# The second layer's expert gate multiplied into the expert rows, and a final stage of gathers and two adds per tile

## The chip, the cores and the metric

The kernel runs on one core of one Trainium2 chip. The metric is the device time of one execution in microseconds. Engines: PE (TensorE, matrix products and transposes), DVE (VectorE), ACT (ScalarE), POOL (GpSimd, which here issues the indirect gathers) and SP (SyncE, which issues plain loads and stores; ACT issues some stores too).

## The reference, cut to what matters

A two-layer backbone over 512 latent and 256 context tokens of width 1024, in float32. Each layer is a mixer (four head groups, an output projection, a gated residual) followed by a mixture of experts. Only latent tokens are needed behind the second layer's mixer. What the change touches is the last residual:

```python
g_top_p, g_top = lax.top_k(g_prob, 1)
e_w = jax.nn.softmax(e_top_l, axis=-1) * g_top_p      # two experts per token
...
out = jnp.zeros((n_tok + 1, d), h.dtype).at[slot_tok].add(y * slot_w[:, None])
...
h_lat = h_lat + mod_l[5] * y_lat.reshape(bsz, n_lat, d_model)
```

`mod_l[5]` is a vector of 1024 gates, one per column, the same for all latent tokens. So a token's result is its residual plus gate times (w0 y0 + w1 y1), where y0 and y1 are the rows that its two experts give.

## The kernel before, in words

The residual `hT` is kept transposed in SBUF: 128 of the 1024 columns lie on the partitions in each of DC = 8 blocks, the tokens along the free axis. A tile is 128 tokens; layer 0 has 6 of them, layer 1 puts out 4. `PS` is PSUM with 8 banks of 512 floats. Each engine runs its own program, written out in Python; semaphores, `S(name)`, order them. What is told here is layer 1.

**Routing (L1219 to L1243, L1693 to L1707, L2290 to L2370).** PE transposes the normalized tokens tile by tile (L1234), ACT copies each to `ftok` and stores it as rows in DRAM (`f_rows`; L1699, L1703). Meanwhile DVE works out which row of which expert each token goes to; PE's slot matmuls (L1241) turn that into the list `slots` (L2362). ACT's exponentials (L1706, L1707) go into the routing weights `wtok` (L2365 to L2370). SP holds the third expert's weight load until `wtok` is ready (L814 to L820).

**Experts (L1253 to L1324, L1709 to L1748, L2372 to L2398).** 15 items, one to each expert position before the last, of two or three sub-blocks of 32 rows each, 40 sub-blocks in layer 1. For each item POOL gathers its token rows from `f_rows` (L2492) and PE transposes them (L1265). Per sub-block g: PE multiplies with the gate and up weights (64 matmuls, L1284); ACT takes the silu (L1722) and DVE multiplies (L2383); PE transposes that (L1294) and DVE copies it (L2389); PE multiplies with the down weights (32 matmuls, L1307) into bank 5 + g % 2; ACT copies the result into `ysb` (L1729, in `y_store`) and, after an item's last sub-block, stores it to `y_rows` in DRAM (L1736). The stages are staggered: in PE's loop step g stand gate/up of g, the transpose of g - 1 and the down product of g - 2. SP loads 6 MB of weights for each expert, through three buffers for gate/up and two for down, each load held until the products of the buffer's last user are through.

**Overflow (L1333 to L1359, L1754 to L1766, L2404 to L2414, L2498 to L2506).** A loop that runs at least once takes one block of 128 rows for tokens that found no place: gather, transposes, 32 matmuls of 512 columns (L1344), silu, multiply, transposes (L1349), 16 matmuls (L1355), two copies of 512 columns from banks 5 and 6 into `ysb`, one on ACT (L1761), one on DVE (L2413), and a store (L1764).

**Combine (L1361 to L1375, L2416 to L2439, L2511 to L2518).** For each tile, POOL gathers the two rows y0 and y1 of each token out of `y_rows` into a pair of buffers `r12`, two pairs in all, so from tile 2 on it waits for `hup`. DVE scales one (L2428) and adds the other scaled (L2429); PE transposes the sum (8 transposes, L1371); DVE adds each 128x128 block, times its gate column `mod4[:, L, 40 + c, 0]`, onto `hT` (8 operations, L2435).

**Output (L1396 to L1404, L1779 to L1783, L2454 to L2458, L834 to L839).** After all tiles of `combine`, PE transposes `hT` back (8 transposes per tile, L1402), ACT and DVE each copy one half (L1783, L2458) into `restok`, which has two buffers, and SP stores the tile (L837) and waits for the landing.

At the kernel's start SP loads two tables, `consts` and `cols`, each on a semaphore of its own.

## Time and profile before

| | us |
|---|---|
| median of 3 runs | 2084.05 (2080.42 to 2088.05) |
| the profiled execution, its own time | 2082.55 |
| its span, first to last instruction | 2080.7 |
| busy in the span: PE, DVE, ACT | 1833.0 (88%), 794.7 (38%), 583.0 (28%) |
| moved by DMA | 361.38 MB, mean 174 GB/s |

How to read the views used below. Times in a view are microseconds from the span's start unless marked ns. The *chain* is the work that ended last, followed back: start, length, what; "issue" is time for which the profile shows no cause. The *waits* list engine, its line and tile, what it waited for: total, times, longest. A *timeline* row has start, length (of the merged run of instructions), engine, line, operation, output tile <- input tiles, shapes, count, and in brackets the idle time before it with what ended it. A row of a *line group by form* has line, engine, operation, tiles, shapes, count, then busy us, mean ns of one, and the idle time before. A *window* row has the stretch and its length, then busy us (and instructions) of PE, PE's weight loads, DVE, ACT and POOL, then the granted PE clock (1.00 is 2.4 GHz, 0.50 is 1.2 GHz), the busy share of the DMA engines and the GB/s that they moved. "SPq" and "ACTq" are the sequencers that issue DMAs.

### The profile page before, as it was taken

Reading aid. Unit: us, or ns where it says so; the run is one execution under the profiler, and the core shown is the slowest. Engines: PE = TensorE matmul, PEld = TensorE weight load, DVE = VectorE, ACT = ScalarE, POOL = GpSimd, SP = SyncE. Lnnn points to the kernel's source line nnn. Section 1 sums busy time; section 2 is a strip of 40 time slices with the busy share of each in tenths; the row PEclk is TensorE's granted clock in tenths of the full one; section 3 lists DMA queues with packets and bytes.
Section 4 is the critical chain, followed back from the end, with each engine's and each line's share of the span. In section 5 each row is a group of like instructions: output and inputs, shape, how many; then the busy total and the mean of one; then the engine's idle time right before and its main releaser. Section 6 shows DMA issues by size and latency. Waiting matters only on the chain.

```text
span 2080.7 us, 36365 instructions
## 1 busy us (share of the span) xinstructions
PE 1833.0 (88%) x15671; PEld 1153.4 (55%) x15671; DVE 794.7 (38%) x1692; ACT 583.0 (28%) x1232; POOL 84.8 (4%) x74
## 2 busy tenths in 40 slices
PE   5999999889899879999995699999799886999773
PEld 3454658666545645555542355468466764555432
DVE  2433457578821521111103442356678233111003
ACT  2213223467611311111110313233577231111100
POOL 0000000100100000000001000000100000000001
PEclk9899999999999879999997799999899997999986
DMA  9541101290252677799986112101000438999953
GB/s 365 200 142 53 31 1 51 73 293 20 81 202 87 260 244 285 258 314 348 385 321 243 42 34 94 31 1 51 21 2 12 153 108 277 368 386 380 388 211 131
DMA packets 198591, 361.38 MB, mean 174 GB/s; under 512 B 12216, under 2 KB 74176, under 8 KB 198176
## 3 DMA queue, kind: packets, MB, share of 16 engines
q1 hardware_dynamic: 175696, 316.31, 42.9%
q0 software_dynamic: 6736, 23.99, 3.6%
q10 hardware_dynamic: 16000, 18.75, 2.5%
q8 instruction: 125, 2.05, 0.4%
q14 instruction: 34, 0.28, 0.0%
HBM read 318.26 MB, written 40.77 MB: 173 GB/s over the span
## 4 chain that ended last, share of the span: by engine, by line
PE 75%; DVE 11%; DMA 5%; ACT 5%; SPq 3%; issue 2%; POOL 0%; ACTq 0%; POOLq 0%; DVEq 0%
PE ps L916 14%; PE ps L1284 14%; PE ps L1307 7%; PE ps L1184 7%; PE ps L901 6%; PE ps L1026 4%; PE ps L1060 3%; PE ps L1085 2%; PE ps L866 2%; PE ps L1344 2%; ACT arena L1628 1%; PE ps L1265 1%; SPq L792 1%; DMA arena<-in_moe_w_up 1%; PE ps L885 1%
## 5 line engine op out<-in xcount | busy, mean ns | idle before, releaser
L1284 PE MATMUL ps<-arena 128*32 128x256 f32 x6080 | 352.9, 385 | 13.2 <-DMA arena<-in_moe_w_up 11.8
L916 PE MATMUL ps<-arena 128*128 128x256 f32 (+2 forms) x1056 | 349.1, 486 | 0.9 <-ACT arena L1502 0.9
L1284 PEld LDWEIGHTS ps<-arena 128*32 128x32 f32 x6080 | 203.1, 112 | 146.4 <-issue 20.5
L916 PEld LDWEIGHTS ps<-arena 128*128 128x128 f32 x1056 | 199.0, 191 | 130.5 <-issue 116.4
L2383 DVE TENSOR_TENSOR arena<-ps,arena 128x128 f32<-128x128 f32 x95 | 27.7, 291 | 495.3 <-ACT arena L1722 495.3
L1307 PE MATMUL ps<-arena 128*32 128x256 f32 x3040 | 183.3, 382 | 1.7 <-DVE arena L2389 1.5
L1184 PE MATMUL ps<-arena 128*128 128x256 f32 (+1 forms) x512 | 143.4, 434 | 2.0 <-DVE arena L2075 2.0
L901 PE MATMUL ps<-arena 128*128 128x256 f32 (+1 forms) x384 | 130.8, 501 | 11.8 <-ACT arena L1441 11.6
L1026 PE MATMUL ps<-arena 32*128 32x256 f32 (+5 forms) x528 | 132.9, 513 | 8.9 <-ACT arena L1628 4.9
L1628 ACT ACTIVATE arena<-ps,att_small 128x768 f32<-128x768 f32 (+2 forms) x160 | 123.1, 772 | 19.7 <-DVE att_small L1994 16.5
L1307 PEld LDWEIGHTS ps<-arena 128*32 128x32 f32 x3040 | 89.9, 110 | 62.3 <-DVE arena L2389 1.8
L1184 PEld LDWEIGHTS ps<-arena 128*128 128x128 f32 x512 | 96.6, 190 | 47.0 <-issue 36.6
L1994 DVE TENSOR_REDUCE att_small<-ps 128x1 f32<-128x768 f32 (+1 forms) x128 | 110.8, 887 | 29.4 <-PE ps L1026 28.2
L1722 ACT ACTIVATE arena<-ps 128x128 f32<-128x128 f32 x95 | 26.3, 277 | 311.5 <-PE ps L1284 311.5
L901 PEld LDWEIGHTS ps<-arena 128*128 128x128 f32 x384 | 73.8, 194 | 70.9 <-issue 60.4
L1060 PE MATMUL ps<-consts,arena 128*128 128x128 f32 x560 | 83.9, 287 | 25.6 <-DVE arena L2016 17.0
L1502 ACT ACTIVATE arena<-ps 128x256 f32<-128x256 f32 (+2 forms) x66 | 31.8, 485 | 237.6 <-PE ps L916 227.1
L1640 ACT ACTIVATE arena<-ps 128x512 f32<-128x512 f32 (+1 forms) x132 | 71.9, 544 | 93.8 <-PE ps L1060 92.5
L1060 PEld LDWEIGHTS ps<-consts,arena 128*128 128x128 f32 x560 | 62.9, 144 | 59.3 <-DVE arena L2016 28.3
L1026 PEld LDWEIGHTS ps<-arena 32*128 32x128 f32 (+2 forms) x528 | 61.2, 193 | 55.3 <-issue 38.3
L1729 ACT ACTIVATE arena<-ps 128x256 f32<-128x256 f32 x95 | 36.4, 383 | 168.1 <-PE ps L1307 168.1
L2194 DVE SCALAR_TENSOR_TENSOR hT<-ps,modcol,hT 128x256 f32<-128x256 f32 x40 | 18.6, 482 | 118.8 <-PE ps L1184 118.8
(342 smaller groups left out, 2039.1 us busy)
## 6 DMA issues: line engine op xcount, KB each, us to landing
arena<-in_moe_w_gate SPq DMA_DIRECT2D x32, 2048.0 KB
arena<-in_moe_w_up SPq DMA_DIRECT2D x32, 2048.0 KB
arena<-in_moe_w_down SPq DMA_DIRECT2D x32, 2048.0 KB, 13.5
arena<-in_w_mod SPq DMA_DIRECT2D x24, 2048.0 KB, 17.8
y_rows<-zeros_t SPq DMA_DIRECT2D x2, 9216.0 KB
arena<-in_w_in SPq DMA_DIRECT2D x6, 2048.0 KB, 7.9
arena<-in_w_in SPq DMA_DIRECT2D x8, 1024.0 KB, 5.7
y_rows<-arena ACTq DMA_DIRECT2D x76, 96.0 KB
```

What stands on the lines that cost most here:

```text
L866: last = pe.matmul(PS[32 * g:32 * g + 32, mod_banks(i)[0] + i % 2, :], silu_c[mod_part(i)][:, 32 * kk:32 * kk + 32], mod_w(i)[:, kk * 512: ...
L901: last = pe.matmul(PS[:, 2 * (m % 2) + bk, 0:b - a], wbuf[:, j % 2, c, mm * P:(mm + 1) * P], aT[:, c, a:b], start=(c == 0), stop=(c == DC ...
L916: last = pe.matmul(PS[:, 4 + k % 2, 0:ch[2]], aT[:, c, t * P:(t + 1) * P], wbuf[:, j % 2, c, 0:ch[2]], start=(c == 0), stop=(c == DC - 1))
L1026: ins = pe.matmul(PS[:, regions(u)[k] + o // 512, o % 512:o % 512 + w], qh, kh, start=True, stop=True, skip_group_check=True)
L1060: last = pe.transpose(PS[:, b, x * P:(x + 1) * P], prob(u, k)[:, c * P:(c + 1) * P], ident)
L1085: last = pe.matmul(PS[HD * k:HD * k + HD, b, o:o + w], p[:, vc, v0:v0 + HD], probT(u, k)[:, c, 0:w], start=(c == 0), stop=(c == nk - 1), s ...
L1184: last = pe.matmul(PS[:, 4 + n % 2, 0:b - a], wo(c, m), oT[:, c, a:b], start=(c == 0), stop=(c == DC - 1))
L1284: last = pe.matmul(PS[32 * q:32 * q + 32, 2 + g % 2, 0:2 * P], xT(k % 2)[:, a:a + SUB], gate_up_cols(r, c, q), start=(c == 0), stop=(c == ...
L1307: last = pe.matmul(PS[32 * q:32 * q + 32, 5 + g % 2, 0:2 * P], hidT_g(g)[:, c * SUB:(c + 1) * SUB], wd[:, c, q * 2 * P:(q + 1) * 2 * P], s ...
L1628: last = act.activation(prob(u, k)[:, x * w:(x + 1) * w], src[:, x * w:(x + 1) * w], ACT.Exp, bias=att_cols(0, u, k)[:, x:x + 1], accum_ou ...
L1640: ins = act.activation(dst, src.rearrange("p (c n) -> p c n", c=dst.shape[1]), ACT.Copy)
L1994: dve.tensor_reduce(att_cols(0, u, k, 1), v, AX.X, ALU.max, negate=True).then_inc(S("nm_done"), 1)
```

## The change

In layer 1 alone:

- PE lays the gate vector out over all partitions, by multiplying each gate column, broadcast, with the identity: as a full row of 1024 (banks 0 and 1) and in the layout of a sub-block's down product (bank 2). ACT copies both to SBUF (`gate_row`, `gate_sub`). PE and DVE wait for them (`gates_ready`) before their expert loops.
- The copy of each down product moves from ACT to DVE and becomes a multiply with `gate_sub`. In the overflow block DVE does both halves, each a multiply with `gate_row`. ACT still issues the stores.
- PE no longer runs `combine`. Right after the overflow block it transposes `hT` back, all four tiles into the eight banks of PSUM.
- POOL gathers all eight sets of rows without waiting, into buffers of their own (`y_pair`).
- DVE, per tile: PSUM plus y1 times its weight, then plus y0 times its weight, into one of four `restok` buffers; SP stores the tile. ACT has no part in it.

Besides, the two tables' semaphores become one, and each of their waits waits for both tables. Layer 0 is otherwise as it was.

```diff
+        restok = ar(A_F, 4 * D).rearrange("p (b n) -> p b n", b=4)
+        gate_sub = ar(M_X + 4 * D + 14 * P, 2 * P)
+        gate_row = rows[:, 0:D]
+        def y_pair(i, k):
+            return ar(M_GU[1] + (2 * i + k) * D, D)
...
             for i in range(NT - CT):
-                sp.wait_ge(S("tok_a"), NT + i + 1)
                 sp.wait_ge(S("tok_d"), NT + i + 1)
-                sp.dma_start(out[0, i * P:(i + 1) * P, :], restok[:, i % 2, :]).then_inc(S(f"f_out{i % 2}"), 16)
+                sp.dma_start(out[0, i * P:(i + 1) * P, :], restok[:, i, :]).then_inc(S(f"f_out{i % 2}"), 16)
...
+                if L == LAYERS - 1:
+                    pe.wait_ge(S("ftok_a"), OT0[L] + T)
+                    for c in range(DC):
+                        g = mod4[:, L, 40 + c, 0:1]
+                        pe.matmul(PS[:, c // 4, (c % 4) * P:(c % 4 + 1) * P], bc(g, (0, P)), ident, start=True, stop=True,
+                                  skip_group_check=True)
+                        q = c // 2
+                        last = pe.matmul(PS[32 * q:32 * q + 32, 2, (c % 2) * P:(c % 2 + 1) * P], bc(g, (0, 32)), ident,
+                                         start=True, stop=True, skip_group_check=True)
+                    last.then_inc(S("ftok_ps"), 1)
...
-                combine(L)
-            pe.wait_ge(S("h_final"), LAYERS)
+                if L == 0:
+                    combine(L)
             for i, t in enumerate(out_tiles(1)):
-                if i >= 2:
-                    pe.wait_ge(S("tok_a"), NT + i - 1)
-                    pe.wait_ge(S("tok_d"), NT + i - 1)
                 for c in range(DC):
-                    last = pe.transpose(PS[:, 2 * (i % 2) + c // 4, (c % 4) * P:(c % 4 + 1) * P],
-                                        hT[:, c, t * P:(t + 1) * P], ident)
+                    last = pe.transpose(PS[:, 2 * i + c // 4, (c % 4) * P:(c % 4 + 1) * P], hT[:, c, t * P:(t + 1) * P], ident)
...
+                if L == LAYERS - 1:
+                    act.wait_ge(S("ftok_ps"), OT0[L] + OTN[L] + 1)
+                    act.activation(gate_row, PS[:, 0:2, :].rearrange("p b n -> p (b n)"), ACT.Copy)
+                    act.activation(gate_sub, PS[:, 2, 0:2 * P], ACT.Copy).then_inc(S("gates_ready"), 1)
                 act.wait_ge(S("rt_in"), L + 1)
...
+                def y_gated(g):
+                    k, sub = SUBS[L][g]
+                    dve.wait_ge(S("dn_ps"), g0 + g + 1)
+                    if sub == 0:
+                        dve.wait_ge(S(f"y_out{k % 2}"), 16 + 16 * stores(L, k))
+                    dve.tensor_tensor(ysb(k % 2)[:, sub * 256:(sub + 1) * 256], PS[:, 5 + g % 2, 0:256], gate_sub, mul
+                                      ).then_inc(S("y_a"), 1)
...
                     if g >= 1:
                         h_evac(g - 1)
+                    if L == LAYERS - 1 and g >= 2:
+                        y_gated(g - 2)
...
+                        dve.tensor_tensor(ysb(par)[:, 0:512], PS[:, 5, :], gate_row[:, 0:512], mul)
+                        dve.tensor_tensor(ysb(par)[:, 512:], PS[:, 6, :], gate_row[:, 512:], mul).then_inc(S("t_dve"), 1)
...
             for i, t in enumerate(out_tiles(1)):
                 dve.wait_ge(S("tok_ps"), NT + i + 1)
-                if i >= 2:
-                    dve.wait_ge(S(f"f_out{i % 2}"), 16 * (NT // 2 + (NT - CT) // 2 + i // 2))
-                dve.tensor_copy(restok[:, i % 2, 512:], PS[:, 2 * (i % 2) + 1, :]).then_inc(S("tok_d"), 1)
+                dve.wait_ge(S(f"g_in{i}"), 32 * (NT // 2 * (i < 2) + 1))
+                o = restok[:, i, :]
+                link(dve.scalar_tensor_tensor(out=o, in0=y_pair(i, 1), scalar=wtok[:, NT + t:NT + t + 1],
+                                              in1=PS[:, 2 * i:2 * i + 2, :].rearrange("p b n -> p (b n)"), op0=mul, op1=ALU.add))
+                dve.scalar_tensor_tensor(out=o, in0=y_pair(i, 0), scalar=wtok[:, t:t + 1], in1=o, op0=mul, op1=ALU.add
+                                         ).then_inc(S("tok_d"), 1)
...
-                    if i >= 2:
-                        pool.wait_ge(S("hup"), OT0[L] + i - 1)
+                    if L == 0 and i >= 2:
+                        pool.wait_ge(S("hup"), i - 1)
                     for k in range(TOPK):
                         pool.indirect_dma_start(
-                            out=r12(i, k), out_offset=None, in_=dram["y_rows"],
+                            out=y_pair(i, k) if L else r12(i, k), out_offset=None, in_=dram["y_rows"],
                             in_offset=bass.IndirectOffsetOnAxis(ap=dest[:, k * NT + t:k * NT + t + 1], axis=0)
-                        ).then_inc(S(f"g_in{i % 2}"), 16)
+                        ).then_inc(S(f"g_in{i if L else i % 2}"), 16)
```

## Rows read from the trace of the kernel before

**Rows 1.** The chain of waits, from the last weight loads to the end.

```profile
1955.16 23.76 DMA arena<-in_moe_w_up
...
2032.31 2.72 DMA y_rows<-arena
...
2035.99 0.94 POOL arena L2515
...
2037.24 5.39 DMA arena<-y_rows,dest
...
2043.42 0.03 issue
...
2056.67 6.38 DMA arena<-y_rows,dest
...
2069.55 3.69 PE ps L1402 x16
...
2076.79 0.69 DVE arena L2458
```

**Rows 2.** Window over the last part of layer 1's expert loop.

```profile
1950.00:1993.00 43.00, 35.87 (x551) 21.61 (x551) 4.16 (x15) 4.73 (x14) 0.00 (x0) 0.92 1.04 393
```

**Rows 3.** Waits of ACT in layer 1's expert loop.

```profile
ACT arena L1729 <- PE ps L1307: 72.1, 40, 2.8
```

**Rows 4.** Line groups by form, DVE.

```profile
L1989 DVE TENSOR_TENSOR ps<-ps,arena 128x256 f32<-128x256 f32 x32 | 13.7, 429 | 2.5 <-PE ps L1026 2.3
...
L2429 DVE SCALAR_TENSOR_TENSOR arena<-arena,wtok 128x1024 f32<-128x1024 f32 x10 | 12.8, 1284 | 0.4
...
L2409 DVE TENSOR_TENSOR arena<-ps,arena 128x512 f32<-128x512 f32 x2 | 1.4, 691 | 34.1 <-ACT arena L1759 34.1
```

**Rows 5.** Timeline of one sub-block of layer 1's expert loop, PE and DVE.

```profile
1770.04 3.64 PE L1284 MATMUL ps<-arena 128*32 128x256 f32 x64
...
1774.05 0.29 DVE L2383 TENSOR_TENSOR arena<-ps,arena 128x128 f32<-128x128 f32 x1 [5.01 <-ACT arena L1722]
```

**Rows 6.** Timeline of the overflow block's end and the gathers, DVE and POOL.

```profile
2031.44 0.69 DVE L2413 COPY arena<-ps 128x512 f32<-128x512 f32 x1 [7.23 <-PE ps L1355]
...
2039.73 0.94 POOL L2515 DMA_INDIRECT arena<-y_rows,dest  x1 [0.31 <-issue]
...
2049.22 1.20 POOL L2515 DMA_INDIRECT arena<-y_rows,dest  x1 [8.56 <-DVE hT L2435]
```

**Rows 7.** Timeline of layer 1's routing, PE, ACT, DVE and SP.

```profile
1717.88 1.95 PE L1234 MATMUL ps<-consts,arena 128*128 128x128 f32 x8
...
1721.30 1.02 ACT L1699 ACTIVATE arena<-ps 128x1024 f32<-128x1024 f32 x1 [0.89 <-DMA f_rows<-arena]
...
1722.71 1.28 ACT L1706 ACT_TABLE_LOAD   x1 [0.39 <-ACT arena L1699]
...
1732.43 3.63 PE L1241 MATMUL ps<-arena 128*128 128x36 f32 x16 [12.61 <-DVE arena L2357]
...
1736.29 0.16 DVE L2365 TENSOR_REDUCE arena<-arena 128x4 f32<-128x16 f32 x1
...
1738.30 0.39 SPq L792 DMA_DIRECT2D arena<-in_moe_w_gate  x1
```

**Rows 8.** Windows over layer 1's routing and the start of its experts.

```profile
1716.00:1720.00 4.00, 3.25 (x14) 2.85 (x14) 2.28 (x10) 0.61 (x1) 0.00 (x0) 0.50 1.04 412
1720.00:1732.00 12.00, 0.00 (x0) 0.00 (x0) 10.90 (x35) 3.04 (x5) 0.00 (x0) 0.50 0.71 288
1744.00:1748.00 4.00, 4.00 (x56) 2.25 (x52) 0.00 (x0) 0.03 (x1) 0.00 (x0) 0.69 1.05 324
```

**Rows 9.** Windows over the data of the first four gathers.

```profile
2041.00:2044.00 3.00, 0.00 (x0) 0.00 (x0) 1.31 (x2) 0.00 (x0) 0.00 (x0) 0.50 0.95 351
2044.00:2045.00 1.00, 0.21 (x1) 0.21 (x2) 0.73 (x1) 0.00 (x0) 0.00 (x0) 0.50 0.47 193
```

**Rows 10.** The chain of waits in layer 0's combine, first pair of gathers.

```profile
1108.44 8.52 DMA arena<-y_rows,dest
```

More of the change, by code:

```diff
@@ L1725, in y_store @@
                     k, sub = SUBS[L][g]
-                    act.wait_ge(S("dn_ps"), g0 + g + 1)
-                    if sub == 0:
-                        act.wait_ge(S(f"y_out{k % 2}"), 16 + 16 * stores(L, k))
-                    act.activation(ysb(k % 2)[:, sub * 256:(sub + 1) * 256], PS[:, 5 + g % 2, 0:256], ACT.Copy
-                                   ).then_inc(S("y_a"), 1)
+                    if L == 0:
+                        act.wait_ge(S("dn_ps"), g0 + g + 1)
+                        if sub == 0:
+                            act.wait_ge(S(f"y_out{k % 2}"), 16 + 16 * stores(L, k))
+                        act.activation(ysb(k % 2)[:, sub * 256:(sub + 1) * 256], PS[:, 5 + g % 2, 0:256], ACT.Copy
+                                       ).then_inc(S("y_a"), 1)
                     n = it[k][2]
@@ L1760, in experts @@
                     act.wait_ge(S("t_pe"), 4 * o + (2 * L + 6))
-                    act.activation(ysb(par)[:, 0:512], PS[:, 5, :], ACT.Copy).then_inc(S("t_act"), 1)
+                    if L == 0:
+                        act.activation(ysb(par)[:, 0:512], PS[:, 5, :], ACT.Copy).then_inc(S("t_act"), 1)
+                    else:
+                        act.sem_inc(S("t_act"), 1)
                     act.wait_ge(S("t_act"), 3 * o + 3)
@@ L1778, in _ @@
                 experts(L)
-            for i, t in enumerate(out_tiles(1)):
-                act.wait_ge(S("tok_ps"), NT + i + 1)
-                if i >= 2:
-                    act.wait_ge(S(f"f_out{i % 2}"), 16 * (NT // 2 + (NT - CT) // 2 + i // 2))
-                act.activation(restok[:, i % 2, 0:512], PS[:, 2 * (i % 2), :], ACT.Copy).then_inc(S("tok_a"), 1)
         @block.vector
```

30 lines of the change are left out of this document (20 added, 10 removed).

## The prediction

> **What bounds the kernel now.** The profile was read from its end backwards, because nearly all of the edit works in the last 50 us. The busy table says little here: PE is busy 88% of the whole span, but the end is another stage with another limit.
>
> The chain of waits [rows 1] shows the last stretch as a ladder of hand-overs. The store of the last block of expert rows takes 2.72 us to land. The first gather is issued at 2035.99, the second at 2037.24, and both have landed 5.39 us later, at 2042.63. Then each tile is scaled and added on DVE, transposed on PE and added to the residual on DVE. From tile 2 on, a gather waits for that residual add of two tiles before. The last pair (second gather issued at 2056.67) needs 6.38 us to land. Only behind all four tiles come the transposes of the result (3.69 us in the chain) and their copies, which share two buffers with the stores. The last copy starts at 2076.79 and takes 0.69, so it ends at 2077.48; the span ends at 2080.70. What lies behind the last copy is 3.22 us.
>
> The stage before it, layer 1's experts, is set by the weight stream. In 1950 to 1993 the DMA engines are busy all the time at 393 GB/s while PE is busy 35.87 of 43 us [rows 2], and the chain there has a piece of 23.76 us of waiting for up weights [rows 1]. What the edit changes inside that stage matters only if it costs more than PE's slack, or holds back a load.
>
> **Part 1: the gate goes into the rows as they leave PSUM.** In the loop over layer 1's 40 sub-blocks the copy of the down product (ACT, L1729) becomes a multiply on DVE. ACT's copies always waited for PE (72.1 us over 40, none for a store) [rows 3]. The DVE multiply should cost what another 128x256 multiply out of PSUM costs, 429 ns (L1989) [rows 4]. DVE is idle 5.01 us before its next hidden-state multiply, in a sub-block that stands for the 40 [rows 5]; 0.43 fits in. Queued behind the new wait on DVE are the hidden-state multiply and the transposed copy of the next sub-block; PE's down product ends some 3.6 us before the gate/up product (3.64 us for its 64 matmuls, [rows 5]) that the next multiply needs. I take 0. If the cover were gone it would be 40 x 0.43 = 17 us.
>
> In the overflow block (one pass here) two 128x512 halves, copied side by side before (one on ACT, one on DVE), are multiplied one behind the other on DVE: 0.69 more (L2409, 691 ns, [rows 4]; the copy that it replaces starts at 2031.44 and is also 0.69, [rows 6]). This lies on the path: +0.70.
>
> Making the gate tiles: 16 matmuls on PE behind the fourth copy of the token rows, then two ACT copies ahead of the exponential. The fourth copy ends at 1721.30 + 1.02 = 1722.32. Eight transposes of that size take 1.95 us at the slow clock, 0.24 each, and a slot matmul (3.63 for 16) starts every 0.23 but, taken one by one, lasts 0.41, so 16 take between 3.9 and 6.6 us and end by 1728.9. Two copies (1.02 and some 0.4) end by 1730.3, and the table load (1.28) with the exponentials by 1732.1. PE's next job, the slot matmuls, starts at 1732.43, and DVE first needs the exponentials at 1736.29 [rows 7]. So all of it is hidden behind DVE's routing work, with 3.5 us to spare on PE and 4.2 on ACT. Cost 0, with a possible gain: PE's granted clock is 0.50 (1.2 GHz) from 1720 to 1732, where PE stands still, and in 1744 to 1748, after steady work, it is on the way up (0.69) [rows 8]. If the new matmuls bring it to 2.4 GHz and it holds, the 3.6 us of slot matmuls shrink by up to 1.8, and since the weight stream starts at 1738.30 behind the routing weights [rows 7], the whole expert stage moves up by as much. Bounds: -1.8 to 0; I take 0, as a burst of 3.25 us just before (1716 to 1720) left the clock at 0.50 [rows 8].
>
> **Part 2: residual transposed during the last store.** PE is free once both multiplies are done, at 2032.14 + 0.70 = 2032.8. The 32 transposes at the slow price of 0.24 take 7.8 us and end at 2040.6, before the first pair lands (2042.63 + 0.70 = 2043.3). So their 3.69 us leave the path. Without this cover they would cost at most that again.
>
> **Part 3: eight gathers in one run.** Issue spacing is 1.25 us (2035.99, 2037.24) and held for four in a row, the fourth at 2039.73 [rows 1, 6]. Eight are issued by 2036.7 + 8 x 1.25 = 2046.7. What decides is the data. Four gathers, 4 x 128 rows of 4 KB or 2.10 MB, are through by about 2044.5; once running they move 351 GB/s [rows 9]. The other four go on at that rate: 2.10 MB / 351 = 6.0 us. Alone, the last would land at 2044.5 + 0.7 + 6.0 = 2051.2. But from about 2047 on the output stores of finished tiles run beside it. Layer 0 shows what sharing does: with weight loads beside it, the same first pair took 8.52 us instead of 5.39 [rows 1, 10]. The first store is issued at 2046.0 (below) and moves data about a microsecond later. By 2047.1, 2.10 + 1.9 x 0.351 = 2.77 MB of the gathers' 4.19 are in, and 1.42 MB are left; if each queue gets half of the 393 GB/s that the weight stream reaches [rows 2], that is 7.2 us: 2054.3. So the last pair lands between 2051.2 and 2054.3; I take the middle, 2052.7, as the stores fill only part of that time. A straggling share of the engines, as in the last pair before (6.38 against 5.39), can add up to 2.
>
> The Trainium skill, "DMA: Bandwidth & Descriptors", section "Queues, rings and completion order", states that an engine takes turns between its queues, packet by packet. That rule speaks against the edit, whose stores of early tiles now cut into the late gathers. The layer-0 row agrees with it; by the rule alone the sum would take its upper end, 2054.3.
>
> **Part 4: two adds per tile.** Gone: the scaling, PE's transposes of the combined tile, eight residual adds and the copies. New: one scalar-times-tensor-plus-tensor of 128x1024 with PSUM as addend, one from SBUF. The latter is 1284 ns (L2429) [rows 4]. The former is in no row; SBUF at 1.28 is one end, two 512-wide PSUM operations (2 x 0.69 = 1.38) the other; I take 1.30. With 0.03 from one DVE instruction to the next [rows 1], a tile is 2.65 us. Adds alone, from 2043.36: four tiles end at 2053.96. The last tile behind its gathers: 2052.7 + 2.65 = 2055.35. The later counts. The four adds that go with the PSUM operand could each differ by 0.1, and only the last tile's is on the path.
>
> The gather that ran beside DVE's scaling took 1.20 us to issue against 0.94 alone [rows 6], and the edit takes that scaling away. The Trainium skill, "SBUF — State Buffer", section "Who interferes with whom", says why: a one-source DVE operation in its two-port mode shuts GpSimd out of their shared port, and a two-input operation does so only against reads. By it, the new run of gathers keeps 0.94; without it, the last two issues lose up to 0.3 each, which the data rate hides.
>
> The merged start semaphore and the same-sized rest of layer 0 cost nothing: the first transposes wait for the inputs, which are loaded later on the same queue.
>
> **Sum.** Last tile done 2055.35, and 3.22 behind it (store and its landing; the stores before it are through by then): 2058.6 against 2080.7, a gain of 22.1 us. The profiled execution took 2082.55 for its span of 2080.70, so 2060.4 for that one. The runs' median is 2084.05, 1.5 above it, so I forecast 2084.05 - 22.1 = 2062.
>
> **Rivals.**
> *The adds bind, not the data.* If stores and gathers do not hurt each other, the end of the adds is 2053.96 (data: 2051.2 + 2.65 = 2053.85), the gain 2080.7 - 2057.2 = 23.5: 2060.5. For it: the weight stream's 393 GB/s show that 351 is not all the engines can move [rows 2, 9]. Chance 0.17.
> *The clock helps the routing.* 1.8 more on top of the forecast: 2060.2. For: new PE work shortly before the slot matmuls; against: 3.5 to 6 us of idleness between. Chance 0.15.
> *The gathers do not run ahead.* The edit then does not do what it says. If GpSimd could only issue a pair when the one before has landed, each pair costs 0.94 + 0.30 + 6.4 = 7.7: the last lands at 2043.3 + 23 = 2066.4, end 2072.3, gain 8.4: 2075.6. Against it: four went out with no gap. Chance 0.05.
> *The expert loop pays, and more than the tail gives.* DVE, held in the new multiply, delivers the next hidden state late and PE waits in each of 40 sub-blocks. One full multiply each time, 17 us, would leave 2084.05 - 22.1 + 17 = 2079. Slower than before by over 0.3% it gets from (22.1 + 6.3) / 40 = 0.71 us a sub-block; at 0.8 it would be 2094. Against it stand the 5.01 us of idleness and a stage set by loads. Chance 0.03 for the slower side, 0.04 for a loss that leaves no change.
> The forecast itself has 0.56.
>
> **Range.** Around 2062: below it adds that bind (-1.5), the clock (-1.8) and the spread of the runs, 2080.42 to 2088.05 (-3.6), together 2055.1; above it full sharing (+1.6), a straggler (+2) and the spread (+4.0), together 2069.6. As these hardly all meet, 2055.5 to 2069. Left out are 0.05 below, and above it the serial gathers and the paying loop, 0.12. A measurement of this kernel tells some 0.3%, 6.3 us, from no change. Faster 0.93 (forecast, adds, clock, serial gathers), same 0.04, slower 0.03.
>
> **What would show it.** Right: eight gathers in the GpSimd row 1.25 apart, no wait between them; 32 transposes before the first pair lands; four tiles of two adds, 1.3 each, the last behind "DMA arena<-y_rows"; the last tile done some 19 us after the first gather. The slot matmuls start where they did. The length of the expert stage, from the first weight load to the start of the overflow block, unchanged within 2 us. Wrong: gaps before gathers five to eight, PE waiting for DVE in the down product, DVE waiting for stores, or adds over 1.4.

## The result and the profile after

The changed kernel's median is 2065.47 us (2061.15 to 2067.03), the kernel before's beside it 2084.60. The ratio is 0.9901, with a 95% interval of 0.9882 to 0.9919: about 20.6 us, or 1%, faster (the two medians alone differ by 19.1). A second measurement (`after_again`, below) gave 0.9908 (0.9893 to 0.9922). Forecast were 2062 and a gain of 22.1.

The profiled execution of the changed kernel took 2066.86 us, its span 2065.0; that is 15.7 less than the 2080.7 of before. The chain of waits, from the overflow block's multiplies to the end (start, length, what), answers to [rows 1]:

```profile
2037.57 0.07 DVE arena L2446
...
2038.18 0.69 DVE arena L2447
...
2039.04 2.72 DMA y_rows<-arena
...
2042.72 0.94 POOL arena L2553
...
2051.41 7.76 DMA arena<-y_rows,dest
...
2059.26 1.29 DVE arena L2493
...
2060.57 1.28 DVE arena L2495
```

The ladder is gone: one run of gathers, the landing of its last member, two adds, the store. From the first gather's issue to the end of the span it is 2065.0 - 2042.72 = 22.28 us, against 2080.70 - 2035.99 = 44.71 before [rows 1]. I call this the last stretch. It gave 22.4 us. But everything in front of it came later: the first gather is issued 6.7 us later than before. Where these 6.7 went can be read at fixed points of the two traces. Timeline of the changed kernel's routing (compare [rows 7]):

```profile
1712.62 1.07 PE L1229 MATMUL ps<-consts,arena 128*128 128x20 f32 x8 [0.52 <-DVE arena L2257]
...
1725.20 1.02 ACT L1712 ACTIVATE arena<-ps 128x1024 f32<-128x1024 f32 x1 [0.84 <-DMA f_rows<-arena]
...
1726.28 0.80 PE L1245 MATMUL ps<-consts,modcol 128*128 128x128 f32 x2 [2.80 <-ACT arena L1712]
1727.01 0.64 PE L1248 MATMUL ps<-consts,modcol 128*32 128x128 f32 x2
...
1734.81 1.22 DVE L2372 TENSOR_TENSOR arena<-arena,consts 128x1024 f32<-128x1024 f32 x1
...
1736.06 0.64 PE L1248 MATMUL ps<-consts,modcol 128*32 128x128 f32 x2
1736.62 3.63 PE L1256 MATMUL ps<-arena 128*128 128x36 f32 x16
```

- The first matmul of layer 1's routing starts at 1712.62, in the kernel before at 1708.99. These 3.6 us are lost before any edit of layer 1 runs, and they are not the edit's: the second trace of the changed kernel has this matmul at 1709.34, the second trace of the kernel before has it at 1712.20. In the same way the last stretch begins at 2036.85 in the second trace of the changed kernel, 5.9 us earlier than in the first, and at 2039.53 in the second trace of the kernel before, 3.5 later than in its first.
- The slot matmuls start at 1736.62 although DVE was through at 1734.81 + 1.22 = 1736.03. PE was still at the gate matmuls (L1245, L1248), which took from 1726.28 to 1736.6, 10.3 us. The slot matmuls start 0.59 behind DVE, against 0.05 in the kernel before: 0.5 us of the edit's own.
- The expert loop is 1.6 us longer in this trace than in that of the kernel before (1.5 longer than in the second trace of the same changed kernel), the stretch from its end to the last down product 0.4.
- The overflow block's two multiplies in a row cost 0.6: L2446 from 2037.57, L2447 from 2038.18.

Timelines of the last stretch, first PE, then DVE, then POOL (compare [rows 6]); a row of several instructions has their merged length:

```profile
2039.20 3.71 PE L1416 MATMUL ps<-consts,hT 128*128 128x128 f32 x32 [1.67 <-DVE arena L2447]
...
2049.31 1.28 DVE L2493 SCALAR_TENSOR_TENSOR arena<-arena,wtok,ps 128x1024 f32<-128x1024 f32 x1 [10.45 <-DMA arena<-y_rows,dest]
2050.63 1.28 DVE L2495 SCALAR_TENSOR_TENSOR arena<-arena,wtok 128x1024 f32<-128x1024 f32 x1
2052.74 1.28 DVE L2493 SCALAR_TENSOR_TENSOR arena<-arena,wtok,ps 128x1024 f32<-128x1024 f32 x1 [0.82 <-DMA arena<-y_rows,dest]
...
2059.26 1.28 DVE L2493 SCALAR_TENSOR_TENSOR arena<-arena,wtok,ps 128x1024 f32<-128x1024 f32 x1 [1.24 <-DMA arena<-y_rows,dest]
...
2050.16 0.94 POOL L2553 DMA_INDIRECT arena<-y_rows,dest  x1 [0.30 <-issue]
2051.41 1.31 POOL L2553 DMA_INDIRECT arena<-y_rows,dest  x1 [0.31 <-issue]
```

DVE waits for gathers ahead of three of its four tiles, 12.5 us in all, 10.45 of them ahead of the first. The transposes of the residual end at 2042.9, before any row of the gathers moves (0 GB/s from 2042 to 2044). Windows over the stretch (columns as in [rows 9]):

```profile
2048.00:2052.00 4.00, 0.00 (x0) 0.00 (x0) 2.57 (x2) 0.00 (x0) 3.08 (x4) 0.50 0.91 310
2052.00:2056.00 4.00, 0.00 (x0) 0.00 (x0) 3.14 (x3) 0.00 (x0) 0.72 (x1) 0.50 0.99 365
2056.00:2060.00 4.00, 0.00 (x0) 0.00 (x0) 2.73 (x3) 0.00 (x0) 0.00 (x0) 0.50 1.02 418
```

The DMA engines are full, up to 418 GB/s, while DVE has gaps. Up to the last pair's landing the new bound is the data; behind it come one tile's adds and the landing of its store.

### The profile page after: what moved, and what is told of

Read it like the earlier page. It is cut to its first block, busy times and chain, and to the rows that moved or that the text cites. A ratio compares the mean times of both kernels' runs of the same rounds, so it can differ in the third digit from the quotient of the medians.

```text
span 2065.0 us, 36321 instructions
## 1 busy us (share of the span) xinstructions
PE 1837.9 (89%) x15671; PEld 1150.8 (56%) x15671; DVE 802.9 (39%) x1696; ACT 566.1 (27%) x1189; POOL 84.5 (4%) x74
## 4 chain that ended last, share of the span: by engine, by line
PE 74%; DVE 9%; DMA 5%; ACT 5%; SPq 4%; issue 2%; POOL 0%; ACTq 0%; POOLq 0%; DVEq 0%
PE ps L920 15%; PE ps L1301 14%; PE ps L1324 7%; PE ps L1188 7%; PE ps L905 6%; PE ps L1030 5%; PE ps L1064 3%; PE ps L1089 2%; SPq L797 2%; PE ps L870 2%; PE ps L1361 2%; ACT arena L1641 1%; PE ps L1282 1%; PE ps L889 1%; DMA arena<-y_rows,dest 1%
## 5 line engine op out<-in xcount | busy, mean ns | idle before, releaser
L2530 POOL DMA_INDIRECT arena<-f_rows,slots x33 | 30.3, 920 | 721.2 <-PE ps L1282 435.0
## 6 DMA issues: line engine op xcount, KB each, us to landing
arena<-in_moe_w_up SPq DMA_DIRECT2D x32, 2048.0 KB, 20.5
```

## The experiments

Theory 1 is the prediction's: the ladder's serial work per tile was the cost, the new end is set by gathers with stores beside them, then one tile's adds and a store. Its first rivals: that the early gathers alone pay; that the adds bind; that the expert loop pays.

**b_gathers_run: the kernel before with the eight gathers in one run.**

```diff
-                    if i >= 2:
-                        pool.wait_ge(S("hup"), OT0[L] + i - 1)
+                    if L == 0 and i >= 2:
+                        pool.wait_ge(S("hup"), i - 1)
...
-                            out=r12(i, k), out_offset=None, in_=dram["y_rows"],
+                            out=y_pair(i, k) if L else r12(i, k), out_offset=None, in_=dram["y_rows"],
```

> The kernel before with one part of the change alone: layer 1's eight gathers in one run, into eight buffers of their own; all else as before. Theory 1 (the gain comes from the work taken off the serial ladder of each tile, not from the gathers): DVE stood idle only 0.73 and 0.66 us for tiles 2 and 3, so 1.4 us are gained, 2083 against 2084.6, with the time from the first gather to the end falling from 44.7 to 43.3 us. Rival (the early gathers are what pays): the ladder shortens by 5 us or more, below 40 us.

Measured: the last stretch is 2080.6 - 2038.07 = 42.5 us, 2.2 less than the first trace of before and 1.4 less than the second (`before_again`, 43.97). Timeline of DVE in b_gathers_run:

```profile
2044.44 0.75 DVE L2434 TENSOR_SCALAR arena<-arena,wtok 128x1024 f32<-128x1024 f32 x1 [10.23 <-DMA arena<-y_rows,dest]
...
2050.65 0.75 DVE L2434 TENSOR_SCALAR arena<-arena,wtok 128x1024 f32<-128x1024 f32 x1
...
2056.85 0.75 DVE L2434 TENSOR_SCALAR arena<-arena,wtok 128x1024 f32<-128x1024 f32 x1
```

No wait for a gather is left behind the first, and still each tile takes 6.2 us: scale, add, 2 us on PE, eight adds. So the rungs of the ladder, not the gathers' late start, made up the 44 us. The ratio of the whole kernel, 0.9971 (0.9961 to 0.9981), 6 us, is more than this stretch explains; the stretch in front of it is not shorter in the trace. Where the other 4 us come from stays open. The kernel before has a median of 2087.99 beside this one and beside the next three, against 2084.60, 2085.55 and 2085.74 beside the others, so part of it may be that these runs of the kernel before were long.

**a_gathers_paired: the changed kernel with gathers five to eight held.**

```diff
+                    if L == 1 and i >= 2:
+                        pool.wait_ge(S("tok_d"), NT + i - 1)
```

> The changed kernel with gathers five to eight held as in the kernel before: those of tile i wait for the adds of tile i - 2. Theory 1: now that a tile takes only 2.6 us on DVE, the gathers are what a tile waits for, so holding them costs: the third pair is issued when the first tile is done (9.2 us after the first gather), lands 7.6 later, the fourth follows some 3.5 behind, and the time from the first gather to the last add grows from 19.1 to 23.0 us; 3.9 us slower than the changed kernel. Rival (the adds bind anyway, the run of gathers is idle decoration): within 1 us of the changed kernel.

Measured: from the first gather (2039.13) to the last add's end (2062.57) 23.4 us, to the end of the span 26.6; 4.3 us more than the changed kernel. Ratio 0.9915 (0.9893 to 0.9937). Timeline of POOL and DVE:

```profile
2048.54 0.93 POOL L2555 DMA_INDIRECT arena<-y_rows,dest  x1 [4.74 <-DVE arena L2495]
...
2055.13 1.28 DVE L2493 SCALAR_TENSOR_TENSOR arena<-arena,wtok,ps 128x1024 f32<-128x1024 f32 x1 [3.52 <-DMA arena<-y_rows,dest]
```

The same hold that cost 1.4 to 2.2 us in front of the long ladder costs 4.3 in front of the short one. The two halves of the edit belong together.

**a_stores_held: the changed kernel with all stores behind the last gather's landing.**

```diff
+            sp.wait_ge(S("g_in2"), 32)
+            sp.wait_ge(S("g_in3"), 32)
             for i in range(NT - CT):
```

> The changed kernel with all output stores held until the last gather has landed. Theory 1 (stores of finished tiles cut into the gathers): the last pair lands 14.5 us after the first gather is issued instead of 16.4, the adds run through to 17.3 instead of 19.1, but four stores then stand at the end, 2.1 MB at some 390 GB/s and a microsecond of start: 6.6 us behind the last gather's landing, total 1.5 us slower than the changed kernel. Rival (the gathers are slow by themselves when eight run, the stores do them no harm): the last pair still lands at 16.4, and the kernel is 3 us or more slower.

Measured: ratio 0.9902 (0.9879 to 0.9925), which is the changed kernel's. SP issues its first store at 2059.50, when the last gather has landed, 15.0 us after the first gather (2044.45); in the changed kernel that landing comes after 16.4 (2059.16 - 2042.72). So stores beside the gathers do delay them, by 1.4 us. But the last stretch is 2066.6 - 2044.45 = 22.15 us, no longer than the changed kernel's. Theory 1 had it 1.5 longer. Whichever goes first, the end is the same. That points at the sum of the bytes but does not prove it: behind the last landing the DMA engines stand nearly still here for a moment before the stores run. Timeline of SP's queue, then windows over the end:

```profile
2059.50 2.99 SPq L843 DMA_DIRECT2D out<-arena  x4
...
2054.00:2058.00 4.00, 0.00 (x0) 0.00 (x0) 3.54 (x3) 0.00 (x0) 0.40 (x1) 0.50 1.00 400
2058.00:2060.00 2.00, 0.00 (x0) 0.00 (x0) 1.96 (x3) 0.00 (x0) 0.00 (x0) 0.50 0.19 76
```

From 2054 to 2058 gathers move alone, at 400 GB/s: the 351 that the prediction took for them from [rows 9] is not their limit.

**a_gates_late: the wide gate matmuls moved out of the routing.** The eight of the full row stand behind the last down product (into banks 5 and 6), the eight narrow ones stay.

```diff
-                        pe.matmul(PS[:, c // 4, (c % 4) * P:(c % 4 + 1) * P], bc(g, (0, P)), ident, start=True, stop=True,
-                                  skip_group_check=True)
...
                 pe.wait_ge(S("y_a"), g0 + NS[L])
+                if L == LAYERS - 1:
+                    for c in range(DC):
+                        last = pe.matmul(PS[:, 5 + c // 4, (c % 4) * P:(c % 4 + 1) * P], bc(mod4[:, L, 40 + c, 0:1], (0, P)), ident,
+                                         start=True, stop=True, skip_group_check=True)
+                    last.then_inc(S("ftok_ps"), 1)
```

> The changed kernel with the eight matmuls of the full gate row moved out of the routing, to the wait for the overflow block's gather; the eight narrow ones stay. In the changed kernel the sixteen took 10.3 us at the slow clock and the slot matmuls began 0.6 us after they were free to. Theory 1: with eight left (0.65 us each, 5.2 in all) they end 4 us before DVE is ready, the slot matmuls begin within 0.1 us of it, and the stage is 0.5 us shorter; the eight moved ones fit in the 6 us in which PE waits for the gather. 0.5 us faster, not to be told in the total. Rival (the slow clock follows from what PE does here): with a pause of 4 us behind fewer matmuls nothing changes in their pace, or the moved ones delay the overflow block by up to 3 us.

Measured: ratio 0.9869 (0.9848 to 0.9890); the slot matmuls start within 0.1 us of DVE's being ready. What neither theory had is how long the eight take when they are alone. Timeline of PE:

```profile
1723.08 1.10 PE L1246 MATMUL ps<-consts,modcol 128*32 128x128 f32 x16 [2.87 <-ACT arena L1715]
...
1998.04 2.02 PE L1347 MATMUL ps<-consts,modcol 128*128 128x128 f32 x16 [0.64 <-DVE arena L2416]
```

1.10 us for the narrow eight (x16, as each is recorded twice), where 5.2 had been expected, and 2.02 for the wide eight. The granted clock was 0.50 for the narrow and 1.00 for the wide ones, so the sum of 3.1 cannot be set beside the 10.3 as it stands; but a clock half as fast would make it 5.1 at most (an estimate: 1.10 + 2 x 2.02). That made a second theory: the turn from one shape to the other at every step is what costs.

**after_again: the changed kernel once more, beside the next three.**

> The changed kernel itself, beside the kernel before on the same chip, to have its ratio in the session of the next kernel: 0.990 (0.988 to 0.992), and a second trace. From the first gather to the end 22.3 us again if that stretch is as regular as it looks; the gate matmuls end between 0 and 2.6 us after the slot matmuls could have begun, as the three traces with them so far differ by that.

Measured: ratio 0.9908 (0.9893 to 0.9922). Its last stretch is 2059.3 - 2036.85 = 22.45 us, with the landing of the last pair after 16.7. The gate matmuls start at 1722.40 here, the last one at 1732.18, and the slot matmuls at 1732.80, 0.06 behind DVE's 1732.74: no cost.

**a_best: the edit of a_gates_late and three more.**

```diff
+                        if L == LAYERS - 1 and half == 0:
+                            last.then_inc(S("t_half"), 1)
...
+                        dve.wait_ge(S("t_half"), i + 1)
                         dve.tensor_tensor(ysb(par)[:, 0:512], PS[:, 5, :], gate_row[:, 0:512], mul)
+                        dve.wait_ge(S("t_pe"), 4 * o + (2 * L + 6))
...
+                dve.wait_ge(S(f"g_in{i}"), 32 * NT // 2 * (i < 2) + 16)
+                link(dve.scalar_tensor_tensor(out=o, in0=y_pair(i, 0), scalar=wtok[:, t:t + 1],
...
+                dve.wait_ge(S(f"g_sec{i}"), 16)
+                for a, b in ((0, D),) if i < NT - CT - 1 else ((0, D // 2), (D // 2, D)):
```

> The changed kernel with four edits: the eight wide gate matmuls at the wait for the overflow block's gather (as in a_gates_late); in the overflow block the first half is multiplied on DVE as soon as its eight down matmuls are through, beside the other eight; each tile's first add takes the row set gathered first and waits for that gather alone, the second add waits for the other; the last tile's second add and its store go in two halves. Theory 1: 0.6 to 1 us from the routing, 0.6 from the overflow block, up to 1.3 from the split wait (only the second add, 1.28, stands behind the last landing), 0.5 from the halved store: 3 us faster than the changed kernel, ratio 0.9885, and 20.5 us from the first gather to the end instead of 22.3. Rival: the last two gathers land together, so that the split wait gives nothing: 22 us for that stretch, and 1.5 us in all.

Measured: median 2060.95, ratio 0.9888 (0.9870 to 0.9906). The ratio is the one expected, by luck, as the stretch is not. The last stretch is 2058.5 - 2036.51 = 22.0 us, where 20.5 had been expected and 22 was the rival's figure, though for another reason. Timeline of DVE:

```profile
2028.56 0.69 DVE L2457 TENSOR_TENSOR arena<-ps,rows 128x512 f32<-128x512 f32 x1 [3.79 <-PE ps L1376]
2031.99 0.69 DVE L2459 TENSOR_TENSOR arena<-ps,rows 128x512 f32<-128x512 f32 x1 [2.74 <-PE ps L1376]
...
2052.29 1.28 DVE L2505 SCALAR_TENSOR_TENSOR arena<-arena,wtok,ps 128x1024 f32<-128x1024 f32 x1 [1.25 <-DMA arena<-y_rows,dest]
2054.51 1.42 DVE L2509 SCALAR_TENSOR_TENSOR arena<-arena,wtok 128x512 f32<-128x512 f32 x2 [0.95 <-DMA arena<-y_rows,dest]
```

The overflow block gave its 0.6 back: the first multiply runs 3.4 us ahead of the second. The split wait worked as built, the two gathers of a tile do not land together, but the last landing moved from 16.4 us after the first gather to 17.9 (2054.4 - 2036.51): the tiles were done earlier and the first store was issued 7.7 us after the first gather (2044.21) where the changed kernel issues it after 9.2 (2051.94). Since a_stores_held shows that stores delay the gathers, the likely reading is that what DVE gained, the stores ate; no run separates the two.

**a_dve9 and a_dve13: more work on DVE in the expert loop.**

```diff
+                    for _ in range(9):
+                        link(dve.tensor_tensor(ar(ARENA - 512, 256), gate_sub, gate_sub, mul))
```

> The changed kernel with nine more multiplies of 128x256 (SBUF only, result not used) behind each of the 40 gate multiplies on DVE in layer 1's expert loop: some 9 x 0.43 = 3.9 us more per sub-block, which takes 5.6 us on PE and on DVE used 1.0. Theory 1 (DVE's results are needed one whole sub-block later, so only its total per sub-block counts: 4.9 of 5.6): no change, under 2 us. Rival of the prediction (the next hidden-state multiply stands right behind and is late by what exceeds its 3.3 us of idle time, 0.5 us and more in each of 40 sub-blocks): 20 us slower.

> As a_dve9 with thirteen: 5.6 us more, 6.6 us of DVE per sub-block against PE's 5.6. Theory 1 (throughput): DVE now sets the pace, 1 us per sub-block, some 35 to 45 us slower than the changed kernel, less what the wait for weights had left over (about 10 us). If the stage were set by the weights alone and DVE had still more room, nothing would change.

Measured from the slot list to the overflow block's release (the DVE operation that writes `slots`, the POOL copy of `slot`), in us: 257.0 and 257.2 in the two traces of before, 258.6 and 257.1 in the two of the changed kernel, 258.3 with nine more multiplies, 278.5 with thirteen. Nine cost nothing in the loop; thirteen cost 20. The whole kernel with nine: ratio 0.9923 (0.9901 to 0.9944); its 3 us lie behind the loop, between the release and the first gather (46.8 against 43.8 and 43.3), where the extra work of the last sub-blocks delays the overflow block. With thirteen that stretch takes 51.1, and the one execution took 2092.05: 25.5 us above the changed kernel's 2066.53, the lower end of what theory 1 had. Timelines of DVE, first of a_dve9, then of a_dve13:

```profile
1783.13 0.42 DVE L2411 TENSOR_TENSOR arena<-ps,arena 128x256 f32<-128x256 f32 x1 [0.63 <-PE ps L1324]
1783.47 4.08 DVE L2414 TENSOR_TENSOR arena<-arena 128x256 f32<-128x256 f32 x9
1787.59 0.29 DVE L2398 TENSOR_TENSOR arena<-ps,arena 128x128 f32<-128x128 f32 x1
```

```profile
1782.12 0.29 DVE L2398 TENSOR_TENSOR arena<-ps,arena 128x128 f32<-128x128 f32 x1
...
1782.86 5.93 DVE L2414 TENSOR_TENSOR arena<-arena 128x256 f32<-128x256 f32 x13
1788.82 0.29 DVE L2398 TENSOR_TENSOR arena<-ps,arena 128x128 f32<-128x128 f32 x1
```

With nine, DVE reaches its next hidden-state multiply without any idle time, 0.7 us later than it could have, and PE does not mind. With thirteen a sub-block takes 6.7 us (1788.82 - 1782.12) against 5.6, and the waits view of a_dve13 names it:

```profile
PE ps L1311 <- DVE arena L2398: 30.9, 33, 4.5
```

So only DVE's total per sub-block counts. In the loop 4.1 us of added work per sub-block cost nothing, and 5.9 cost 0.5 each (20 over 40). On average a sub-block of the changed kernel takes 6.4 (257 over 40), more than PE's 5.6.

**before_again: the kernel before against itself.**

> The kernel before against itself, to have a second trace of it from the same chip and hour as the later kernels, and to see what the comparison says of no change: ratio 1.000 within 0.002, 44.7 us from the first gather to the end (the kernel with its gathers in one run had 42.5 there, yet its ratio was 0.9971, 6 us, so either this stretch is 48 us on that chip or the rest of the kernel differs by chance). The first gather within 3 us of 2036.

Measured: ratio 0.9995 (0.9983 to 1.0008), last stretch 2083.5 - 2039.53 = 43.97 us. The comparison does not invent 6 us here, so this run does not explain the ratio of b_gathers_run either.

**a_gates_grouped: the wide gate matmuls first, then the narrow ones.**

```diff
                         pe.matmul(PS[:, c // 4, (c % 4) * P:(c % 4 + 1) * P], bc(g, (0, P)), ident, start=True, stop=True,
                                   skip_group_check=True)
+                    for c in range(DC):
+                        g = mod4[:, L, 40 + c, 0:1]
                         q = c // 2
```

> The changed kernel with one order changed: in the routing PE does the eight wide gate matmuls (128 rows out) and then the eight narrow ones (32 rows out), instead of one of each in turn. Theory 2 (what made them 10.3 us is the turn from one shape to the other at each step, 0.73 and 0.57 us apiece, not the clock): the narrow eight alone took 1.10 us in a_gates_late at the same slow clock, the wide eight alone 2.02 late in the stage, so 3.1 to 5.1 us in all; the slot matmuls begin within 0.1 us of DVE's being ready even where the last token copy is late. Rival (the slow clock and the broadcast weights): about 10.3 us again. In the total 0 to 2.5 us, not to be told.

Measured: ratio 0.9889 (0.9866 to 0.9913). Timeline of PE:

```profile
1722.30 3.66 PE L1245 MATMUL ps<-consts,modcol 128*128 128x128 f32 x16 [2.77 <-ACT arena L1714]
1725.89 0.66 PE L1250 MATMUL ps<-consts,modcol 128*32 128x128 f32 x16
1732.14 3.63 PE L1258 MATMUL ps<-arena 128*128 128x36 f32 x16 [5.59 <-DVE arena L2374]
```

The same sixteen in 4.25 us instead of 10.3, with 5.6 us to spare in front of the slot matmuls. Theory 2 holds. The granted clock is no rival: it was 0.50 up to 1725 and rose then (0.65 from 1725 to 1726, 1.00 to 1728), so the narrow eight ran faster, but at 0.50 they had taken 1.10, and 3.66 + 1.10 is still 4.8.

**a_half_gathers: half of the last gathers left out.** The second row set of each token isn't gathered; both adds read the first.

```diff
-                dve.wait_ge(S(f"g_in{i}"), 32 * (NT // 2 * (i < 2) + 1))
+                dve.wait_ge(S(f"g_in{i}"), 32 * NT // 2 * (i < 2) + 16)
...
-                link(dve.scalar_tensor_tensor(out=o, in0=y_pair(i, 1), scalar=wtok[:, NT + t:NT + t + 1],
+                link(dve.scalar_tensor_tensor(out=o, in0=y_pair(i, 0), scalar=wtok[:, NT + t:NT + t + 1],
...
-                    for k in range(TOPK):
+                    for k in range(1 if L else TOPK):
```

> The changed kernel with half of the work of the last gathers left out: only the first of the two row sets of each token is gathered, both adds read it (the output is wrong in that part). 2.1 MB less to move out of 6.3, the same adds and stores. Theory 2 (after the change the last stretch is bound by what the DMA engines must move, gathers and stores together, since five orders of the work all gave 22.0 to 22.5 us from the first gather to the end): the stretch falls until the adds bind: first row set landed after 5.4 us instead of 6.6, adds 10.6, then 3.2: 19.2 to 19.5 us, 3 us less, and DVE runs without a wait from the first add on. Rival (the adds and the first landing bind): 21 us or more.

Measured: ratio 0.9880 (0.9858 to 0.9902); the last stretch falls to 2060.2 - 2042.49 = 17.7 us, 4.6 less with the same adds and stores. Timeline of DVE:

```profile
2046.80 1.28 DVE L2493 SCALAR_TENSOR_TENSOR arena<-arena,wtok,ps 128x1024 f32<-128x1024 f32 x1 [8.17 <-DMA arena<-y_rows,dest]
...
2055.71 1.28 DVE L2495 SCALAR_TENSOR_TENSOR arena<-arena,wtok 128x1024 f32<-128x1024 f32 x1
```

Eight adds in 10.2 us without a gap. Here the adds bind; in the changed kernel they do not. It is 1.5 to 1.8 us shorter than expected, mostly as the first set lands after 4.2 us and not 5.4. The run does two things at once: half the gathers' bytes are gone, and the adds start earlier, at one set's landing instead of two. The adds alone, started where the changed kernel starts them (6.6 us after the first gather), would end the stretch after 6.6 + 10.2 + 3.2 = 20.0 us, an estimate; so the data cost the changed kernel some 2.3 of the 4.6, and the earlier start is the rest.

**a_transposes_late: the cover of the transposes taken away.**

```diff
+            pe.wait_ge(S("g_in0"), 32 * (NT // 2 + 1))
             for i, t in enumerate(out_tiles(1)):
```

> The changed kernel with the 32 transposes of the residual held until the first pair of gathers has landed, so that the cover is gone. Rival to the prediction's price: it said at most 3.7 us. Theory 2: PE's clock has dropped to 1.2 GHz by then, a tile's eight take 2.0 us, the first tile's adds start 2.0 us later, the others run ahead of DVE; since the data set the end and not the adds, the stores only start later and cut less into the gathers: 22.3 to 23 us from the first gather to the end, against 22.3 to 22.5 now. Theory 1 (adds and transposes on the path): 24.3 or more.

Measured, in one execution: last stretch 2062.2 - 2040.18 = 22.0 us. Timelines of PE and DVE:

```profile
2046.93 5.17 PE L1417 MATMUL ps<-consts,hT 128*128 128x128 f32 x32 [11.90 <-DMA arena<-y_rows,dest]
2048.93 1.28 DVE L2494 SCALAR_TENSOR_TENSOR arena<-arena,wtok,ps 128x1024 f32<-128x1024 f32 x1 [12.58 <-issue]
...
2057.79 1.28 DVE L2496 SCALAR_TENSOR_TENSOR arena<-arena,wtok 128x1024 f32<-128x1024 f32 x1
```

The first tile starts 2.0 us later, then DVE never waits, and the end does not move: the adds have room to be late. The room is these 2 us and no more, as DVE works here without a gap from its first add to its last: adds and data end within 0.3 us of each other.

The last stretch in all versions, from the first gather's issue to the end of the span, in us:

| kernel | first gather | span | stretch |
|---|---|---|---|
| before, before_again | 2035.99, 2039.53 | 2080.7, 2083.5 | 44.7, 44.0 |
| b_gathers_run | 2038.07 | 2080.6 | 42.5 |
| after, after_again | 2042.72, 2036.85 | 2065.0, 2059.3 | 22.3, 22.5 |
| a_gathers_paired | 2039.13 | 2065.7 | 26.6 |
| a_stores_held | 2044.45 | 2066.6 | 22.2 |
| a_gates_late | 2038.90 | 2061.3 | 22.4 |
| a_best | 2036.51 | 2058.5 | 22.0 |
| a_gates_grouped | 2036.11 | 2058.6 | 22.5 |
| a_transposes_late | 2040.18 | 2062.2 | 22.0 |
| a_half_gathers | 2042.49 | 2060.2 | 17.7 |
| a_dve9 | 2047.42 | 2070.0 | 22.6 |
| a_dve13 | 2067.98 | 2090.2 | 22.2 |

## Why the prediction was right, point by point

**The ladder.** Right. The stretch behind the first gather was forecast at 2058.6 - 2036.7 = 21.9 us and took 22.3 and 22.5. Eight gathers went out 1.24 us apart with no wait between them. b_gathers_run shows that their early start alone is worth 1.4 to 2.2.

**The last pair's landing.** Right in kind and size: forecast 16.0 us after the first gather (between 14.5 and 17.6), measured 16.4 and 16.7. The stores' share in it, 1.4 us, came out in a_stores_held; the step put it at 1.5 for the middle. Its rate was wrong in detail and right on average: the gathers did not go on at 351 GB/s but started slower (258 from 2044 to 2048, 310 to 2052) and ended faster, with 400 GB/s alone in a_stores_held; alone they landed after 15.0, where the step had 14.5. The Trainium skill, "DMA: Bandwidth & Descriptors", section "Queues, rings and completion order", states turns between queues packet by packet. That stores delay gathers agrees with it, and so does a_best, where stores issued earlier go with a landing at 17.9; the upper end that the prediction worked out by it, 17.6 after the first gather, the changed kernel did not reach.

**The adds.** Right in size: 1.28 for the one out of PSUM (1.30 taken, 1.28 to 1.38 as ends) and 1.28 for the other. Their place was right as well: in the chain the last tile's adds follow the last landing. What the step does not say is that landing and adds are not independent, since finished tiles send out stores: a_best (adds earlier, landing later) and a_transposes_late (adds 2 us later, DVE without a wait) leave the stretch at 22. The rival "the adds bind", with its 2060.5, was wrong: its price assumed that stores and gathers do not hurt each other.

**The overflow block.** 0.70 forecast, 0.6 measured, as the second multiply is issued before the first is out.

**The gate matmuls.** The term that was mis-sized, and the one sign that failed: the slot matmuls did not start where they did. It took 0.24 to 0.41 us for each of the sixteen, 3.9 to 6.6 in all, and left 3.5 us to spare. They took 10.3 (0.80 and 0.64 as the rows show them, 1.29 for a pair from start to start), and nothing was left. Whether it costs depends on when the fourth token copy ends, which waits for a store beside the weight stream: the slot matmuls start 0.05 to 2.56 us behind DVE in the eight traces that have the alternating order (after 0.59, a_stores_held 2.56, after_again 0.06), where 0.05 is what the kernel before has. That cost 0.5 us in the first trace, so the mistake hardly shows in the total. The prices were read from matmuls that all had one shape. A rule of the Trainium skill, "TensorEngine Tiling (Array Packing)", section "Key Properties", speaks of just this, that a change of tiling mode drains the engine; the prediction did not weigh it. The pair of traces with alternating and with grouped order, 10.3 against 4.25 us, agrees with the rule; that draining is the mechanism no row shows.

**The clock.** The hoped-for 1.8 us did not come. The slot matmuls took 3.63 in every version. In the changed kernel the granted clock stayed at 0.50 from 1724 to 1740, though PE was in its alternating matmuls from 1726.3 on (recorded busy for all of 1728 to 1736). In a_gates_grouped the clock did rise before them (0.79 on average from 1724 to 1728), and was back down by the time they ran, 5.6 us after PE's last matmul.

**The expert loop.** Cost taken as 0, measured as 0 within the scatter of a microsecond. The rival's picture, that the multiply's 0.43 us could come through as a wait in every sub-block, was wrong, since DVE's results are due a whole sub-block later; a_dve9 added 4.1 us each in the loop without harm. Its arithmetic, slower by 0.3% from 0.71 us per sub-block, was sound: a_dve13 lost 20 us in the loop and 7.4 behind it, 0.68 for each of the 40, and its one execution came out 0.3% above the kernel before.

**The cover of the transposes.** They took 3.7 us, not 7.8, as PE's granted clock had not yet fallen (1.00 from 2036 to 2044 in the changed kernel), and the cover is worth nothing: without it the end is the same (a_transposes_late).

**The total.** 22.1 us forecast; 20.6 by the ratio of the first measurement, 19.2 by the second. The 6.7 us by which the first trace was late in front of the last stretch are 0.5 of gates, 0.6 of multiplies, and some 5.6 that differ between traces of one and the same kernel too. That the measured median lies only 3.5 us from the forecast is in part luck: single runs of one kernel lie up to 7.6 us apart, and the terms themselves are confirmed by the lengths of stretches, not by the total.

A version that beats the changed kernel beyond doubt isn't shown. a_gates_late (0.9869), a_best (0.9888) and a_gates_grouped (0.9889) all lie below the changed kernel's 0.9901 and 0.9908, by more than the half microsecond or so (in a_best about one) that their traces explain. The intervals of a_best and a_gates_grouped overlap both of the changed kernel's, that of a_gates_late (0.9848 to 0.9890) only the first; but it was measured beside the long runs of the kernel before (2087.99), and its own median of 2060.80 is that of a_best. The grouped order costs two lines and takes away a wait of up to 2.5 us, so it is the one to keep.

## What to carry to other kernels

When a serial ladder is taken away, ask what must still be moved in the stretch that is left: here gathers and stores, 6.3 MB, gave 22 us in whatever order adds, stores and transposes stood, as long as the gathers were issued in one run (held back, they made it 26.6), and only moving less made it shorter. Price small matmuls from rows of the same shape in the same order, and group those of one shape, above all where they stand in front of something that others wait for. A cover that depends on a transfer beside a busy stream is as wide as the worst trace shows, not the one at hand.

## What the runs showed of the hardware

Sixteen matmuls in alternating shapes (128 and 32 rows out, 128 columns) took 10.3 us at the slow clock (granted 0.50); the same in two groups took 4.25, the last 0.66 of it at a rising clock, and 4.8 with the narrow group's price at the slow clock.

Gathers and stores together moved 418 GB/s (2056 to 2060 of the changed kernel). Gathers alone moved 351 where four were under way [rows 9], and 400 towards the end of a run of eight (2054 to 2058 of a_stores_held).

A gather whose issue began while DVE was in an add with both tensors in SBUF took longer, by about what was left of the add less 0.1 (nine traces; the kernel before shows it too, with 1.02 for the gather issued at 2050.73, 0.2 us before L2429 ends, which the prediction did not read): 1.31 us in the changed kernel (L2495 from 2050.63 to 2051.91, the issue at 2051.41), 1.58 in a_gates_late (L2502 from 2047.08 to 2048.36, the issue at 2047.60). Timelines of POOL and then of DVE in a_gates_late:

```profile
2046.36 0.94 POOL L2560 DMA_INDIRECT arena<-y_rows,dest  x1 [0.30 <-issue]
2047.60 1.58 POOL L2560 DMA_INDIRECT arena<-y_rows,dest  x1 [0.31 <-issue]
...
2047.08 1.28 DVE L2502 SCALAR_TENSOR_TENSOR arena<-arena,wtok 128x1024 f32<-128x1024 f32 x1
```

Beside the add with one operand in PSUM it stayed at 0.93 (a_gathers_paired, issue at 2049.78 within L2493 from 2049.01 to 2050.29). The prediction, by the page "SBUF — State Buffer" of the Trainium skill, section "Who interferes with whom", expected 0.94 beside two-input operations too. The page has an operation with two SBUF inputs contend with GpSimd's reads of SBUF, and a gather has its row numbers, `dest`, in SBUF; so the traces do not contradict the page, but the prediction's conclusion from it, that these issues would keep 0.94, failed. Whether the read of `dest` is what waits, no run shows. It cost nothing that the runs can tell, as the data were behind anyway.
